# Level products of the recurrence with only the later half-blocks as moving columns, and predicated copies in place of mask and sum

## What is computed

```python
b = cumsum(logf)                                    # per channel c, over time
decay = where(s <= t, exp(b[t, c] - b[s, c]), 0)
scores[t, s] = sum_c q[t, c] * k[s, c] * decay[t, s, c]
o[t] = sum_s scores[t, s] * v[s] + (q[t] * exp(b[t])) @ state
state = exp(b_last) * state + sum_s (k[s] * exp(b_last - b[s])) outer v[s]
```

## Time and profile before

| | |
|---|---|
| median of 3 runs | 2665.79 us |
| profiled execution | 2666.3 us, span 2664.6 us |
| TensorE busy (matmul) | 2449.2 us, 92% |
| TensorE weight loads | 2203.6 us, 83% |
| VectorE busy | 1903.3 us, 71% |
| ScalarE busy | 1372.1 us, 51% |
| GpSimd busy | 1320.4 us, 50% |
| mean granted TensorE clock | 0.972 |

### The profile page before, as it was taken

The page is one execution under the profiler, slowest core; times in us unless marked ns, Lnnn a source line. Parts: engine busy times, 40 slices in busy tenths (PEclk is TensorE's granted clock), DMA queues, the critical chain, the costliest instruction groups (busy, mean ns, idle before and its releaser), DMA issues. The chain is left out here.

```text
span 2664.6 us, 40711 instructions
## 1 busy us (share of the span) xinstructions
PE 2449.2 (92%) x15142; PEld 2203.6 (83%) x15142; DVE 1903.3 (71%) x3031; ACT 1372.1 (51%) x2032; POOL 1320.4 (50%) x1313
## 2 busy tenths in 40 slices
PE   4999999999999999999986999699999999999980
PEld 4889898898998989989875765599999999999980
DVE  7475765757758567585686797588888888888875
ACT  3443625426245262452633322377777777777772
POOL 6354654646546556465564365344454544554430
PEclk9999999999999999999987999799999999999995
DMA  5201111111111111101113323589999999999986
GB/s 178 65 25 33 51 36 45 34 40 45 42 45 34 40 38 41 53 25 41 44 72 120 103 72 129 145 269 294 298 302 304 298 303 305 301 296 312 360 251 223
DMA packets 207424, 380.80 MB, mean 143 GB/s; under 512 B 22586, under 2 KB 129402, under 8 KB 206714
## 3 DMA queue, kind: packets, MB, share of 16 engines
q1 hardware_dynamic: 180330, 302.31, 33.0%
q0 software_dynamic: 25664, 71.41, 11.9%
q10 hardware_dynamic: 1232, 4.46, 0.5%
HBM read 313.79 MB, written 72.97 MB: 145 GB/s over the span
## 5 line engine op out<-in xcount | busy, mean ns | idle before, releaser
L121 PE MATMUL ps<-xTh,w_mix_low 128*128 128x368 f32 (+1 forms) x1728 | 597.5, 346 | 10.4 <-POOL w_mix_low L115 9.0
L122 PE MATMUL ps<-xTl,w_mix_high 128*128 128x368 f32 (+1 forms) x1728 | 571.0, 330 | 0.0
L123 PE MATMUL ps<-xTh,w_mix_high 128*128 128x368 f32 (+1 forms) x1728 | 568.6, 329 | 0.0
L2055 POOL DMA_INDIRECT ys_d<-yo,tab_early x114 | 214.8, 1884 | 453.0 <-DVE yo L2215 312.6
L121 PEld LDWEIGHTS ps<-xTh,w_mix_low 128*128 128x128 f32 x1728 | 326.9, 189 | 21.8 <-issue 18.5
L122 PEld LDWEIGHTS ps<-xTl,w_mix_high 128*128 128x128 f32 x1728 | 327.1, 189 | 9.1 <-issue 6.2
L123 PEld LDWEIGHTS ps<-xTh,w_mix_high 128*128 128x128 f32 x1728 | 326.7, 189 | 0.0
L2096 PE MATMUL ps<-xghl,wgh 128*128 128x320 f32 (+5 forms) x1024 | 267.3, 346 | 10.4 <-DVE xghl L115 5.9
L2096 PE MATMUL ps<-xghl,wuh 128*128 128x320 f32 (+5 forms) x1024 | 263.5, 344 | 0.0
L2098 PE MATMUL ps<-xghl,wgl 128*128 128x160 f32 (+5 forms) x1024 | 240.6, 235 | 0.0
L2098 PE MATMUL ps<-xghl,wul 128*128 128x160 f32 (+5 forms) x1024 | 238.7, 233 | 0.0
(11 more groups left out here) (369 smaller groups left out, 5945.5 us busy)
## 6 DMA issues: line engine op xcount, KB each, us to landing
wd_early<-in_w_exp_down SPq DMA_DIRECT2D x64, 1024.0 KB, 8.7
wg_early<-in_w_exp_gate SPq DMA_DIRECT2D x124, 512.0 KB, 8.0
wu_early<-in_w_exp_up SPq DMA_DIRECT2D x124, 512.0 KB, 5.4
w_mix_raw<-in_w_in SPq DMA_DIRECT2D x72, 512.0 KB, 3.9
mT_d<-gs_m SPq DMA_DIRECT2D x8, 544.0 KB, 2.7
xr_m<-in_x_prompt SPq DMA_DIRECT2D x8, 512.0 KB, 3.8
xn_d<-xr_m SPq DMA_DIRECT2D x8, 512.0 KB, 2.9
out<-vrow_m SPq DMA_DIRECT2D x8, 512.0 KB, 4.8
```

The source lines that it names most:

```text
L121: pe.matmul(out, ll, rh, start=start, stop=False)
L122: pe.matmul(out, lh, rl, start=False, stop=False)
L123: return pe.matmul(out, lh, rh, start=False, stop=stop)
L2055: pool.indirect_dma_start(out=ys_d[:, :], out_offset=rows_of(e, j, m), in_=yo[:m, b, j, :], in_offset=None, compute_op=ALU.add, bounds_che ...
```

## The change

The level products have as moving columns only the later halves of their blocks (`second_halves`), 64 columns in place of 128 (32 in place of 64 in the short chunk). The stationary side is the same tile as before. The results are as many columns, gathered: column g * w + u of a level is token u of the later half of block g.

VectorE no longer masks and sums. It copies the diagonal under its mask into `aT`, and then each level's columns under that level's mask into the places of the later halves, 8 predicated copies for a full chunk and 7 for the short one. They are chained by a semaphore, `put_s`. `aT` is cleared once at the start, since no copy writes the places with s > t. The tile `pm` is gone. TensorE's products wait for `a_done` in place of `masked`.

```diff
+def second_halves(ap, i):
+    return ap.rearrange("p (g u) -> p g u", u=2 * LEVELS[i])[:, :, LEVELS[i]:2 * LEVELS[i]]
...
-        x, pm = sb("x_m", [P, 2, NL + 1, 256]), sb("pm_m", [P, 2, NL + 1, P])
+        x = sb("x_m", [P, 2, NL + 1, 256])
...
                         if j:
-                            pe.wait_ge(masked, j)
+                            pe.wait_ge(a_done, j)
                         pe.matmul(ps[:m, PB[0], 0:m], kh[:, c0:c0 + m], hq[:, h % 2, c0:c0 + m], start=True, stop=True)
                         for i in SLOT_LEVELS[cn // 2]:
                             xs = x[:, slot, i, xo:xo + m]
                             if 2 * LEVELS[i] <= m:
-                                mm = pe.matmul(ps[:m, PB[(i + 1) // 4], (i + 1) % 4 * P:(i + 1) % 4 * P + m], xs, xs,
-                                               start=True, stop=True)
+                                at = (i + 1) % 4 * P
+                                mm = pe.matmul(ps[:m, PB[(i + 1) // 4], at:at + m // 2], xs, second_halves(xs, i), start=True, stop=True)
...
                     def scores(cn):
                         j, m = NT * h + cn, rows(cn)
-                        s = NL + 1 if m == P else NL
                         dve.wait_ge(p_done, j + 1)
-                        if j >= 2:
-                            dve.wait_ge(a_done, j - 1)
-                        pp = ps[:m, PB[0]:PB[1] + 1, :].rearrange("p b (l t) -> p (b l) t", l=4)[:, 0:s, 0:m]
-                        dve.tensor_tensor(pm[:m, j % 2, 0:s, 0:m], pp, masks[:m, 0:s, 0:m], ALU.mult).then_inc(masked, 1)
-                        dve.wait_ge(masked, j + 1)
+                        if j == 0:
+                            dve.wait_ge(memo, 4)
                         if j >= 2:
                             dve.wait_ge(y_done, j - 1)
-                        dve.tensor_reduce(aT[:m, j % 2, 0:m], pm[:m, j % 2, 0:s, 0:m].rearrange("p l t -> p t l"), AX.X,
-                                          ALU.add).then_inc(a_done, 1)
+                        out = aT[:m, j % 2, 0:m]
+                        put(dve.copy_predicated(out, masks[:m, 0, 0:m].bitcast(U32), ps[:m, PB[0], 0:m]))
+                        levels = [i for i in SLOT_LEVELS[cn // 2] if 2 * LEVELS[i] <= m]
+                        for i in levels:
+                            later, mask = (second_halves(ap, i) for ap in (out, masks[:m, i + 1, 0:m].bitcast(U32)))
+                            at = (i + 1) % 4 * P
+                            step = dve.copy_predicated(later, mask, ps[:m, PB[(i + 1) // 4], at:at + m // 2].rearrange(
+                                "p (g u) -> p g u", u=LEVELS[i]))
+                            if i < levels[-1]:
+                                put(step)
+                        step.then_inc(a_done, 1)
...
-                ch = Chain(dve, entry_s)
+                ch, put = Chain(dve, entry_s), Chain(dve, put_s)
...
+                dve.memset(aT[:, :, :], 0.0).then_inc(memo, 1)
```

More of the change, by code:

```diff
@@ L360, in mixer @@
                        "z_done abs_done e_done l_done z_copied sp_raw sp_done hi_done lo_done c_done arg_raw arg_done w_done o_done "
-                       "osb_copied pa pd diff_done exp_done eb_done qe_exp qe_done x_done p_done masked a_done ke_done ke_copied "
+                       "osb_copied pa pd diff_done exp_done eb_done qe_exp qe_done x_done p_done put_s a_done ke_done ke_copied "
                        "y_done oT_copied su_done s_done sg_done silu_done g_done squares root_ready u_raw merged wo_in wo_high wo_low last_s par_in xr0 xr1 xr2 xr3 var_ready rstd_ready entry_s shift_ready normed scaled xn_ready turned x_high x_low xs0 xs1 xs2 xs3 "
@@ L365, in mixer @@
                 z_done, abs_done, e_done, l_done, z_copied, sp_raw, sp_done, hi_done, lo_done, c_done, arg_raw, arg_done, w_done, o_done,
-                osb_copied, pa, pd, diff_done, exp_done, eb_done, qe_exp, qe_done, x_done, p_done, masked, a_done, ke_done, ke_copied,
+                osb_copied, pa, pd, diff_done, exp_done, eb_done, qe_exp, qe_done, x_done, p_done, put_s, a_done, ke_done, ke_copied,
                 y_done, oT_copied, su_done, s_done, sg_done, silu_done, g_done, squares, root_ready, u_raw, merged, wo_in, wo_high, wo_low, last_s,
@@ L569, in scores @@
                             if h:
-                                pe.wait_ge(masked, NT * h)
+                                pe.wait_ge(a_done, NT * h)
                         if n >= 2:
```

## The result

The changed kernel takes 2688.88 us, the median of 4 runs (2685.32 to 2692.32), against 2665.65 us of the kernel before (4 runs, 2663.15 to 2666.83): a ratio of 1.0089, with the 95% interval 1.0077 to 1.0101. That is 23 us slower, where the forecast was +1.6 us and the range ended at 2676.5. The profiled execution is the quickest of the four, 2685.32 us with a span of 2683.6 us, 19.0 us over the span before.

The account below looks back on a forecast made before the run. TensorE, busy for 92% of the span, was taken to bound the kernel. Terms: -4.2 (products) + 6.1 (wait at chunk 1) - 0.3 (last head) = +1.6 us, forecast 2667.4 us (+0.06%), range 2660 to 2676.5 us.

Parts of the forecast that it names:

- The clock: "Nothing": TensorE's idle time at chunk 1, grown to 2.0 us, leaves the granted clock at 1.00: no cost.
- TensorE: -4.2 us: Level products: half the moving columns save 4.2 ns a record, as the unchanged weight load fills the time; -4.2 us.
- rival 1: Level products: the moving columns decide their time, -50 us there, 2622 us in all; chance 0.08.
- the 107.6 ns: Distance between records of the router's product L1501, of the same shape, taken for the narrow level products against 111.8 ns.
- The chain at chunk 1: +6.1 us: Chunk 1 of each head: TensorE waits for a 1.99 us chain of 8 copies, 0.76 us longer, in eight heads.
- Rival 4: The later start behind chunk 1 is made up by TensorE's later waits: -4.5 us, 2661.3 us; chance 0.04.
- rival 3: GpSimd holds up the copies at chunk 1: a chain of 2.84 us, +12.9 us, 2674.2 us; chance 0.10.
- Rival 2: Copies at chunk 1 cost what the scan costs: +11.3 us there, +6.8 in all, 2672.6 us; chance 0.12.
- Chunks 2 to 8: no cost: Heads 0 to 6: projections between the groups of products cover the 2 us chain with over 6 us to spare.
- VectorE's own time gives nothing: Recurrence of heads 0 to 6: VectorE falls from 3.25 to 1.99 us a full chunk, without gain.
- The last head's end: -0.3 us: Last head's last chunks, paced by VectorE, whose path is 0.5 us shorter: -0.3 us, between -1 and +1.5.
- Strided moving columns: nothing: Six of seven levels read moving columns with a stride; 64 may take twice their time under cover: no cost.

Follow-up runs that it names:

- the release by bank: Changed kernel, but chunk 1's first four products wait only for the first four copies, the others for the last: 2678.82 us; with 128 moving columns 2667.97 us.
- the runs on full columns: 128 moving columns with a 2.2 us wait: changed kernel with them put back, 2679.44 us; kernel before with 6 masks multiplied again ahead of the release, 2679.21 us.
- the kernel with work in the wait: Changed kernel, with TensorE doing 9 unread products of a constant tile while chunk 1's first product waits for the copies: 2672.87 us, ratio 1.0024.
- other banks: Changed kernel with chunk 1's products in the PSUM banks of the output and the state, so without the wait: 2651.05 us; with 128 moving columns 2654.68 us.

## Why the prediction was wrong

- **The clock: "Nothing".** This is the step that failed, and with it the range: some 20 of the 23 us. It took the earlier trace rows as proof that 2.27 us of idle time leave the clock at 1.00. The row of 1334 to 1338 ends while TensorE still idles, and in the second head above the clock, too, is 1.00 for most of the idle time and falls near its end. The next two stretches of that trace, which were not brought in, say so, and so does a stretch within the second:

```profile
1334.00:1338.00 4.00, 1.42 (x5) 0.49 (x4) 3.90 (x6) 2.54 (x5) 2.90 (x2) 1.00 0.00 0
1338.00:1342.00 4.00, 1.26 (x8) 1.08 (x8) 3.97 (x4) 1.40 (x2) 3.92 (x3) 0.65 0.00 0
1342.00:1346.00 4.00, 1.66 (x5) 1.57 (x6) 3.93 (x9) 1.18 (x4) 2.54 (x4) 0.50 0.00 0
...
1339.20:1339.60 0.40, 0.40 (x3) 0.23 (x2) 0.40 (x1) 0.40 (x1) 0.40 (x2) 0.50 0.00 0
```

  The clock is down from 1339.2 on, 0.8 us behind the end of the 2.27 us of idle time and before the next long wait, of 4.72 us, begins at 1339.6. TensorE had a shorter gap of 0.66 us ahead of it too, at 1334.0, so this is no price for 2.27 us alone; but it took away the ground for "nothing", and a case with the clock lost in some heads, at some 3 us each, belonged among the rivals. Even so the wait was only half of it. The step also treated the narrow products as a matter of issue time, and no term asked what they do to the clock; the release by bank shows that they bring the fall at the old idle time. With the wait priced by the runs on full columns the loss would have been 3.4 us and the kernel inside the range.
- **TensorE: -4.2 us.** The mechanism was right and the size was not: it is about -1.6 us, 0.2 a head. The load binds the products, so rival 1 is out. But the 107.6 ns were misread. The router's group, too, has one short distance, 55 ns behind its first record, and from there on 110 to 113 ns; spread over its 15 distances that looks like 4.2 ns a record. There is no gain per record, only one of some 0.05 us a group, and part of it is given back behind the group. At 1.2 GHz it is the loads that double: those behind the wait stand (3.11 - 0.34) / 13 = 213 ns apart.

```profile
365.18 3.11 PEld L659 LDWEIGHTS ps<-x_m 128*128 128x128 f32 x14
```

- **The chain at chunk 1: +6.1 us.** The mechanism was right, in all eight places, and the size off: the chain is 2.27 us (362.47 to 364.74), not 1.99, and the term is 8 x 1.04 = 8.3 us, within the ends of +5.0 and +11.3. One copy of 128 columns takes 305 ns (285 taken), one of 64 takes 249 ns on average (213 taken). Rival 4 is out: with full columns 1.05 us more of wait make the period of a head 0.9 us longer, so the later start is not made up further on.
- **GpSimd (rival 3).** Out: the seven copies take 1.94 us beside an idle GpSimd and 1.95 beside a busy one. Rival 2 named a chain of over 2.45 us; it stayed below.
- **Chunks 2 to 8: no cost.** Right: no wait for the copies there in heads 1 to 7.
- **VectorE's own time gives nothing.** Right inside the heads but for some 0.1 to 0.2 us each, wrong behind them: from the recurrence's last product to the router's first the changed kernel needs 3.6 us less. The kernels with two passes have 48.6 to 49.4 us there, those with copies 45.5 to 47.4, so some 2 us seem to be the copies'; no run tests it, nor why the changed kernel gets back more.
- **The last head's end: -0.3 us.** The last head took 4.0 us more, 3.2 by the clock behind chunk 1, -0.5 by what each head gives back, and 1.3 us at its end, where its waits are 1.60 and 0.97 us and the clock falls once more. Within -1 to +1.5, but for another reason.
- **Strided moving columns: nothing.** Right as to issue: 111 to 112 ns apart with strides and without. What the stride does to the clock is the open point above.
- **Luck in the rest of the sum.** With the clock kept, in the kernel with work in the wait, the change costs 5.8 us (2672.87 against 2667.03 beside it), inside the range. But errors cancel in that: the wait cost 2.2 us more and the narrow products gave 2.6 less than forecast, while 3.6 us behind the recurrence came back where the forecast had nothing.

The Trainium skill, "TensorE: Matmul & The Clock Gate", section "LDWEIGHTS (loading the stationary operand)", gives P/1.2 ns for a load, 106.7 ns for 128 columns. The loads here stand 111.5 ns apart at 2.4 GHz, 5 ns more, and 213 ns at 1.2 GHz, so the figure is one of the full clock. The 107.6 ns that the prediction set beside it were the misread mean.

## What to carry to other kernels

Fewer moving columns in f32 products that are bound by their weight load buy almost nothing in time (0.2 us of the 168 of a head here) and can cost the clock where an idle gap stands beside them: with the same 1.21 us of idle time, 128 columns kept 2.4 GHz in 8 of 8 heads and 64 columns in 2 of 8. Before such a change, or one that lengthens a wait of the bounding engine, look at the granted clock in the stretches behind the gap and not in the gap, and close the gap first: a projection moved into it, or other banks, gave 10 to 11 us of the 12 to 14 that were gained in all. And a gap of TensorE may be worth filling with products that nobody needs: here 2.2 us of them a head made the kernel 16 us faster.

## What the runs showed of the hardware that was not expected

- The clock falls by parts that repeat. The stretch behind a wait loses nothing, 1.7 us or 3.4 us (a little less where the fall begins before TensorE works again), and in all three kernels with full columns and a wait of 2.2 us it is heads 4 and 8 that fall, each by 1.7 us. The first head fell in none of the kernels. Why these heads is not settled.
- A fall hits products, loads and projections alike: in the second head of the changed kernel the 14 records go from 1.67 to 3.09 us, and in a full-column kernel (head 4 of the kernel with copies and 128 columns) from some 1.73 to 3.13 us.
- A predicated copy from PSUM costs more in the levels with the shortest runs: in every full chunk's chain, as in that of chunk 2 here, the copies of the levels with halves of 1 and 2 tokens take 0.30 us, the others 0.23 us, all with 64 columns:

```profile
380.72 0.30 DVE L1098 COPY_PREDICATED aT_m<-masks,ps 128x64 f32<-128x64 uint32 x1
...
381.32 0.23 DVE L1098 COPY_PREDICATED aT_m<-masks,ps 128x64 f32<-128x64 uint32 x1
```
